# First feed-forward: a second group of seven products in place of wide forms, with PSUM seeded by ScalarE

## What is computed

```python
D_MODEL, SEQ, D_FF = 2048, 256, 5632
h = rmsnorm(x, norm_ffn[l])
x = x + (jax.nn.silu(h @ w_gate[l]) * (h @ w_up[l])) @ w_down[l]
```

## Time and profile before

| | |
|---|---|
| three runs | 2476.24, 2477.52, 2479.26 us |
| profiled execution, first to last instruction (span) | 2474.5 us |
| TensorE busy in the span | 2463.8 us, 11266 matmuls |
| VectorE / ScalarE busy | 2105.3 / 1519.2 us |
| first feed-forward, iterations | ten of 62.17 us, from about 446 to 1068 us |

### The profile page before, as it was taken

The page is one execution under the profiler, slowest core; times in us unless marked ns, Lnnn a source line. Parts: engine busy times, 40 slices in busy tenths (PEclk is TensorE's granted clock), DMA queues, the critical chain, the costliest instruction groups (busy, mean ns, idle before and its releaser), DMA issues.

```text
span 2474.5 us, 28461 instructions
## 1 busy us (share of the span) xinstructions
PE 2463.8 (100%) x11266; PEld 2040.7 (82%) x11266; DVE 2105.3 (85%) x1724; ACT 1519.2 (61%) x1448; POOL 102.3 (4%) x96
## 2 busy tenths in 40 slices
PE   9999999999999999999999999999999999999998
PEld 7888888888888888888888888888888888888887
DVE  6977667988888888978788777777799999999997
ACT  7655556566666666665565565444566667766666
POOL 0000000000000000000000000000000000000000
PEclk9999999999999999999999999999999999999999
DMA  9536446677777777775455556557557777777775
GB/s 324 186 136 235 139 153 207 216 237 235 236 236 237 235 238 238 213 251 192 151 187 172 185 204 221 176 168 247 173 194 230 232 233 232 230 230 231 229 247 161
DMA packets 262756, 524.57 MB, mean 212 GB/s; under 512 B 9248, under 2 KB 9248, under 8 KB 262368
## 3 DMA queue, kind: packets, MB, share of 16 engines
q1 hardware_dynamic: 238976, 474.56, 55.8%
q0 software_dynamic: 22784, 46.62, 10.3%
q10 hardware_dynamic: 864, 1.57, 0.2%
HBM read 478.67 MB, written 2.10 MB: 194 GB/s over the span
## 4 chain that ended last, share of the span: by engine, by line
PE 99%; DVE 1%; DMA 0%; ACT 0%; issue 0%; SPq 0%; ACTq 0%; DVEq 0%
PE acc L862 23%; PE acc L866 23%; PE acc L864 23%; PE misc L862 6%; PE misc L866 6%; PE misc L864 6%; PE acc L879 1%; PE acc L875 1%; PE acc L877 1%; PE misc L907 1%; PE misc L915 1%; PE misc L875 1%; PE misc L879 1%; PE misc L877 1%; PE misc L998 0%; PE misc L978 0%
## 5 line engine op out<-in xcount | busy, mean ns | idle before, releaser
L1917 DVE TENSOR_TENSOR w_lo<-w_raw,w_hi 128x2048 fp32r<-128x2048 f32 (+1 forms) x473 | 1059.9, 2251 | 152.4 <-ACT w_hi L1384 151.0
L1384 ACT ACTIVATE w_hi<-w_raw 128x2048 fp32r<-128x2048 f32 (+1 forms) x473 | 892.0, 1890 | 345.5 <-PE acc L866 227.6
L862 PE MATMUL acc<-w_hi,xt_hi 128*128 128x512 f32 x1132 | 447.1, 395 | 0.2
L866 PE MATMUL acc<-w_hi,xt_lo 128*128 128x512 f32 x1132 | 441.3, 390 | 0.0
L864 PE MATMUL acc<-w_lo,xt_hi 128*128 128x512 f32 x1132 | 440.6, 389 | 0.0
L862 PEld LDWEIGHTS acc<-w_hi,xt_hi 128*128 128x128 f32 x1132 | 212.6, 188 | 44.7 <-issue 1.8
L866 PEld LDWEIGHTS acc<-w_hi,xt_lo 128*128 128x128 f32 x1132 | 212.4, 188 | 44.8
L864 PEld LDWEIGHTS acc<-w_lo,xt_hi 128*128 128x128 f32 x1132 | 212.7, 188 | 42.9
L1917 DVE TENSOR_TENSOR w_lo<-w_raw_more,w_hi 128x2048 fp32r<-128x2048 f32 (+1 forms) x99 | 221.8, 2240 | 30.1 <-ACT w_hi L1384 30.1
L1384 ACT ACTIVATE w_hi<-w_raw_more 128x2048 fp32r<-128x2048 f32 (+1 forms) x99 | 186.3, 1884 | 57.5 <-DVE w_raw_more L1887 15.8
L1891 DVE TENSOR_TENSOR w_raw<-w_raw 128x2048 f32<-128x2048 f32 x80 | 182.7, 2283 | 0.0
(11 more groups left out here) (388 smaller groups left out, 4189.8 us busy)
## 6 DMA issues: line engine op xcount, KB each, us to landing
w_raw<-in_w_in SPq DMA_DIRECT2D x132, 1024.0 KB, 5.1
w_raw<-in_w_ffn_up SPq DMA_DIRECT2D x61, 1024.0 KB, 6.6
w_raw<-in_w_ffn_down SPq DMA_DIRECT2D x42, 1024.0 KB, 5.7
x<-staged POOLq DMA_DIRECT2D x80, 512.0 KB, 6.2
w_raw<-in_w_out SPq DMA_DIRECT2D x32, 1024.0 KB, 5.1
w_raw<-in_w_gate SPq DMA_DIRECT2D x32, 1024.0 KB, 6.2
w_raw<-in_w_down SPq DMA_DIRECT2D x32, 1024.0 KB, 7.3
w_raw<-in_w_up SPq DMA_DIRECT2D x27, 1024.0 KB, 5.2
```

The costliest lines, as they stand in the source:

```text
L862: nc.tensor.matmul(bank, hi[:, j, :], w_hi[:, t % RING, j, :], start=first and j == 0, stop=False, skip_group_check=shared)
L866: end = nc.tensor.matmul(bank, lo[:, j, :], w_hi[:, t % RING, j, :], start=False, stop=last and j == C - 1, skip_group_check=shared)
L1384: nc.scalar.activation(w_hi[:, t % RING, rows], raw_tile(steps[t].slot)[:, rows], ACT.Copy).then_inc(hi_ready, 1)
L1917: nc.vector.tensor_tensor(w_lo[:, t % RING, rows], raw_tile(steps[t].slot)[:, rows], w_hi[:, t % RING, rows].bitcast(F32), ALU.subtract).t ...
```

## The change

- In iterations 1 to 10 of the first feed-forward, K blocks 2 and 3 become a second full group of seven products, Q1 to Q7, on the same banks as P1 to P7. An iteration has 18 steps, 14 x 12 + 4 x 24 = 264 matmuls. VectorE makes eight weight sums, all of full size.
- `beta`, `zeta` and `gamma` no longer start from nothing: ScalarE copies `alpha` into them when P1 and Q1, then P6 and Q6, then P7 and Q7 are done (`seeds`), and the matmuls add on to that. Three matmuls before the loop (`set_bits`) mark those banks as written. VectorE's five additions become two (`second_up`, `first_up`). Silu is applied in the copy out of `beta` and `gamma`.
- x is no longer added to by DMA: ScalarE copies a quarter of x into the `acc` pair (`seed_x`), D adds on to it, and ScalarE copies the pair back to x (`x_back`), at once followed by the seed for the next quarter. `staged` and GpSimd have no part in it.
- Raw slots: seven. The sums of tokens for the second group (`q1_hi`, `q1_lo`) are made in block 0, in place of the wide ones.

```diff
-ORDER_WIDE = "P1 G3 P3 E1 D0 P5 E5 D1 E46 P6 U3 P7 P2 E73 D2 P4 D3".split()
-ORDER_WIDE_LAST = "P1 G3 E1 D0 P5 E5 U3 E46 P6 D1 E73 P2 P7 P4 P3 D2 D3".split()
+ORDER_TWO = "P1 Q1 P5 Q5 D0 P6 Q6 D1 P7 P3 Q7 Q3 D2 P2 P4 Q2 Q4 D3".split()
+ORDER_TWO_LAST = "P1 Q1 P5 Q5 D0 P6 Q6 D1 P7 Q7 P3 Q3 P2 Q2 P4 Q4 D2 D3".split()
...
-RAW_SLOTS = 6
+RAW_SLOTS = 7
+FFN_SLOTS = {1: 7, 2: 6}
...
+    def with_two_groups(order, a_weight, a_col, b_weight, b_col, down_weight, down_row):
...
+            release.update({g + "11": at[g + "4"], g + "12": at[g + "7"],
+                            g + "22": max(at[g + "3"], at[g + "6"] - 1, at[g + "7"] - 1),
+                            g + "21": max(at[g + "2"], at[g + "4"] - 1)})
...
+                sums[at[name]] = Sum(0, mine.slot, other.slot, other.count, at[name] - 1, "N" + name[1], None)
...
@@ GpSimd
-        for i in range(1, NF):
-            for n in range(Q):
-                group_read(pool, ("ffn1_down", i - 1, n))
-                k = n % 2
-                pool.dma_start(x[:, :, n * N:(n + 1) * N], staged[k][:], accum_op=ALU.add).then_inc(staged_added[k], 16)
@@ TensorE
+        def set_bits():
+            for b in range(3):
+                bank_free(b, before["sums1", 1][b])
+                nc.tensor.matmul(misc[:, b, :], xt_hi[:, 0, 0:P], xt_hi[:, 0:2, :], start=True, stop=True)
+        def seeded_iteration(i, after, within=None):
...
+                    pe.wait_ge(x_seeded, Q * (i - 1) + n + 1)
...
+                if name == "P6":
+                    pe.wait_ge(beta_seeded, i)
+                if name == "P7":
+                    pe.wait_ge(zeta_seeded, i)
+                if name == "P4":
+                    pe.wait_ge(gamma_seeded, i)
@@ ScalarE
+        def seed_x(m):
...
+            act.wait_ge(pair_read[pair], count)
+            group_read(act, ("ffn1_down", i - 2, n) if i > 1 else ("down", 3, n))
+            copy(acc[:, pair], x[:, :, n * N:(n + 1) * N]).then_inc(x_seeded, 1)
+        def x_back(i, t, n):
+            pair = pair_of(("ffn1_down", i - 1, n))
+            act.wait_ge(tile_used, t + 1)
+            copy(x[:, :, n * N:(n + 1) * N], acc[:, pair]).then_inc(pair_read[pair], 1)
+            if i < NF - 1 or n == 0:
+                seed_x(Q * (i - 1) + n + 1)
...
                 split(t + LEAD)
-                products_read(1, i, t, name, gate, hid)
+                seeds(i, t, name)
                 if k in TURNS:
                     hid_hi_half(i - 1, TURNS.index(k))
...
                 if name[0] == "D":
-                    stage_quarter(1, i, t, int(name[1]))
+                    x_back(i, t, int(name[1]))
@@ VectorE
                 split(t + LEAD)
-                results_read(1, i, t, name, gate, hid)
+                if k > 0 and order[k - 1] == "Q7":
+                    second_up(i)
+                if k > 0 and order[k - 1] == "Q3":
+                    first_up(i, t)
+                if i < NF - 1 and name == "D3":
+                    gated_sums(i)
                 if k in TURNS:
                     hid_lo_half(i - 1, TURNS.index(k))
```

More of the change, by code:

```diff
@@ L92, in two_ahead @@
         return "P7", "E5", "E73"
-    return ("P7",) if order is ORDER_WIDE_LAST else ()
+    return ()
 def last_of(order, *names):
@@ L1124, in pair_step @@
             products(t, [(banks[letter], hi, lo)], first=new, shared=True)
+        def set_bits():
[3 more added lines that the diff above has]
+        def seeded_iteration(i, after, within=None):
+            stage, order = ("ffn1", i), order_of(1, i)
+            sums_key = (*stage, "sums")
+            alpha, epsilon = pair_banks(pair_of(sums_key))
+            banks = {"1": alpha, "6": alpha, "7": alpha, "5": epsilon, "2": misc[:, 0, :], "4": misc[:, 1, :],
+                     "3": misc[:, 2, :]}
+            for k, name in enumerate(order):
+                t = STEP[stage, name]
+                if name[0] == "D":
+                    n = int(name[1])
+                    key = ("ffn1_down", i - 1, n)
+                    if n == 0:
+                        ht_ready(i - 1)
+                    pe.wait_ge(x_seeded, Q * (i - 1) + n + 1)
+                    products(t, both(pair_banks(pair_of(key)), ht_hi, ht_lo), first=False, shared=True,
+                             between=within and within.get(name))
+                    after(k, name)
+                    continue
+                form = name[1]
+                if name == "P1":
+                    pair_free(sums_key)
+                if name == "P6":
[4 more added lines that the diff above has]
+                    pe.wait_ge(gamma_seeded, i)
+                if form in "5673":
+                    pe.wait_ge(s_lo_done, S_PHASES.index("ffn1" if name[0] == "P" else "ffn1q") + 1)
+                    s_hi, s_lo = (s1_hi, s1_lo) if name[0] == "P" else (q1_hi, q1_lo)
+                    hi, lo = s_hi[:, S_FORMS["P" + form]], s_lo[:, S_FORMS["P" + form]]
+                else:
+                    b = (0 if form == "1" else 1) + (0 if name[0] == "P" else 2)
+                    cs, rows = slice(C * b, C * b + C), second if form == "4" else first
+                    hi, lo = xt_hi[:, cs, rows], xt_lo[:, cs, rows]
+                products(t, [(banks[form], hi, lo)], first=name in ("P1", "P5"), shared=True)
+                after(k, name)
         def ffn_iteration(ffn, i, s_hi, s_lo, ready, after, within=None):
@@ L1143, in ffn_iteration @@
                         ready(i - 1)
-                    products(t, both(pair_banks(pair_of(key)), *((ht_hi, ht_lo) if ffn == 1 else (h2_hi, h2_lo))),
-                             between=within and within.get(name))
+                    products(t, both(pair_banks(pair_of(key)), h2_hi, h2_lo), between=within and within.get(name))
                 else:
@@ L2513, in _ @@
             if k == 5:
-                wide_lo_piece(2)
+                wide_lo_piece(1)
                 taps_on(0, "a", 0)
```

170 lines of the change are left out of this document (123 added, 47 removed).

## The result

The changed kernel takes 2502.53 us (median of four runs, 2502.37 to 2503.73) against 2477.46 before: a ratio of 1.0102, 95% interval 1.0088 to 1.0117. It is slower, as forecast, but by 25 us and not by 7. The span of the profiled execution is 2501.8 us, 27.3 more than before; that is more than the 25 of the medians, because the profiled execution was here the slowest of the four (2503.73 us) and, by its span, the fastest (2476.24 us) of the kernel before.

The account below looks back on a forecast made before the run. The prediction took TensorE to bound the kernel, with VectorE having about 10% left. Its terms, -13.6 + 0.7 + 19.5 + 0.6 = +7.2 us, moved the median from 2477.5 to 2484.7, range 2472 to 2498.

Parts of the forecast that it names:

- TensorE's saving: Six matmuls fewer in each of ten iterations, 60 at 0.2267 us: -13.6 us.
- VectorE's sum: VectorE's own work in one iteration of the changed kernel: 60.9 us, against TensorE's 60.8.
- The loop through D1: Gate product, half turn, D1, copy to x, seed, Q3's rounding, VectorE's work to the next gate product: 62.98 us per iteration.
- the second rival: The seed is cheap or partly overlaps: iteration near 62.2, result 2474 to 2482, no change that can be told; chance 0.18.
- The failed step: TensorE's wait of 2.17 us at the first half turn, in nine iterations: +19.5 us.
- The fourth rival: TensorE's clock falls at its 2.2 us stands: up to 2.7 us more each, 2509; chance 0.05 together with the fifth rival.
- Iteration 1: Gate product ends at 447.6, the turn comes at 448.6, so the first iteration was to have no wait.
- The last iteration: In its own order P4's remainder comes at 42.4, TensorE reaches it at 41.8: one more delay, +0.6 us.
- The other loops: Paths through D0, D2, D3 and the seeds of `beta`, `zeta`, `gamma`, taken as shorter than the one through D1.
- D1's load: D1's weight tile takes D0's slot at 7.2 and is wanted at 12.6; landing at 12.8 was to cost nothing.
- the third rival: D1's load lands late in some or all iterations: up to 9 x 2.3 us more, 2490 to 2506; chance 0.12.
- the fifth rival: The saving of TensorE's matmuls isn't there: +13.6 us, 2498; chance 0.05 together with the fourth rival.

Follow-up runs that it names:

- e4: The kernel before, with five of the six matmuls of step E5 left out in each of ten iterations: 2465.03 us against 2477.03.
- e2: The changed kernel with nine idle matmuls ahead of TensorE's wait at the first half turn, iterations 2 to 10: 2489.55 us, ratio 1.0051.
- e8: The changed kernel with two idle matmuls ahead of TensorE's wait at the first half turn: 2489.78 us, ratio 1.0049.
- e10: The changed kernel, with ScalarE's copy to x and seed after D1, D2 and D3 moved behind the next rounding: 2507.35 us, ratio 1.0120.
- e7: The changed kernel, with VectorE's weight sums for P4 and Q4 cut to 64 columns: 2484.13 us, ratio 1.0028.
- e3: The changed kernel, with VectorE making the gate product before the sum for Q5 and the remainder of P5: 2488.98 us, ratio 1.0046.
- e5: The changed kernel, with VectorE's gate product and the first half of `ht_lo` both made earlier: 2487.51 us, ratio 1.0042.
- e13: The changed kernel, with copies to x, seeds and VectorE's sums for P4 and Q4 all cut to 64 columns: 2476.35 us, ratio 0.9997.
- e6: The changed kernel, with gate product and first half of `ht_lo` earlier, and D2's seed behind Q3's rounding: 2482.97 us, ratio 1.0023.
- e1: The changed kernel, with D2's seed of x moved behind the rounding of Q3 on ScalarE: 2485.33 us, ratio 1.0032.

## Why the prediction was wrong in size and right in direction

- *TensorE's saving*, -13.6: right (e4: 0.23 per matmul by the iteration, 0.24 by the medians, where 0.2267 was taken).
- *VectorE's sum*, 60.9: right (61.08 in the windows).
- *The loop through D1*, 62.98: right but for 0.18 (63.16 in e2 and e8, where the clock stays up). The copies of 1.03, the idle time of 2.0 at Q3, the wait of 2.17 (measured 2.13) are all there. The seed, which the trace of before did not have, measured 0.97 from start to start, near the 0.92 taken and far from both of its bounds; the second rival's cheap seed is out. (In the walk, 25.71 and a copy of 1.03 make 26.74 and not 26.76, which changes nothing.)
- *The failed step* is the price of that wait. "TensorE waits 62.98 - 60.81 = 2.17 at the turn" was put into the sum as 2.17 and no more. The matmuls behind it were costed at 0.2267 each, a spacing measured where TensorE never stands. The runs show 0.43 for over 3 us behind each of the nine stands: 1.57 us more each, 14 us in all. The fourth rival said so and priced it well, up to 2.7 an iteration and 2509 in all; it was given a share of 0.05 with another, and the range ended at 2498. The rows of before had no wait of this length, so they bore on it in neither direction, and a chance so small had nothing behind it. With the 14 us the forecast would have been 2499; the wait of iteration 1 (2.1) and the loop's 0.18 nine times (1.6) bring it to the measured 2502.5. That the direction came out right owes nothing to the clock: the loop of 63.16 alone gives the 2489.6 of e2, 0.5% over before. The Trainium skill (TensorE: Matmul & The Clock Gate, Part 1) has the clock fall to half after an idle stretch and come back after sustained work; the windows at 839 to 845 agree, with 0.50 and then 1.00, though not every stand had such a fall behind it (e10).
- *Iteration 1*, "so it does not wait": wrong by 2.1. The time 447.6 was taken from the trace of before, where VectorE makes this product directly behind TensorE's last result; in the changed kernel two weight sums and two remainders stand ahead of it, as the prediction itself says for the other iterations. The hedge in the text ("if they are done before P5") was also a right question. VectorE finishes block 0's token sums at 442.2, makes those four without a gap until 451.0, and ends the product at 452.4. No run tells the share of the token sums from that of the order.
- *The last iteration*, +0.6: measured 0.8.
- *The other loops are "shorter"*: right, but by 0.4 to 0.5 only (D2 alone 62.64 in e7; 62.80 in e3, where TensorE waits for bank 3, and in e5, where it waits at D0). That fits with no single edit that computes everything bringing more than this once the clock was up.
- *D1's load*: ScalarE rounds D1 (851.67) directly behind its copy to `hid` and does not wait for the load; the third rival is out:

```profile
851.10 0.67 ACT L1467 ACTIVATE hid<-acc,rstd 128x512 f32<-128x512 f32 x1
851.67 1.91 ACT L1464 ACTIVATE w_hi<-w_raw_more 128x2048 fp32r<-128x2048 f32 x1
```

- *The saving isn't there*: e4 gained 12.0 us, so the fifth rival is out. The Trainium skill (Perfetto Trace Analysis, Identifying the Most-Contended Engine) would have given e4 no gain as the prediction read it, by weight loads alone; the section names a second measure beside them, the share of the peak FLOPs (MFU), which the prediction left out.

So the large change moves the time the wrong way for reasons of different weight. The copies to x and the seeds stand in ScalarE's queue ahead of roundings (63.16 to 61.84 without their length); the seed is new there, while a copy of the same size, to `staged`, stood there before. VectorE has little slack left to take that up (61.08 of work against TensorE's 60.8), but this weighs less by itself: 4 us less of its work brought 0.52 with the copies in place (e7) and nothing with short ones (e13). And behind the stand that follows, TensorE's clock fell nine times of nine (64.72 against 63.16). The best version that computes everything, e6, is still 0.23% slower than the kernel before.

## What to carry to other kernels

When a change takes work from the bounding engine and puts it on engines with "slack", walk the loop through all of their queues: a signal that goes once around three in-order engines sets the iteration though none of them is full, and next to it lie other loops, nearly as long. Price a new stand of TensorE twice, once for its length and once for the matmuls behind it at half clock, with a chance that is not small. Where such a stand can't be avoided, two idle matmuls in it gave back 13 us here.

## What was not expected of the hardware

- Stands of TensorE of 2.13 us (nine of nine in the kernel after) and 2.23 (one in e3) were followed by matmuls at 1.2 GHz; those of 1.65 to 1.7 (e1, e7, e8) and 1.82 to 2.04 (e3) were not. Among the longer ones it was not the length that decided: of those of 2.08 to 2.19 in iteration 1 three of thirteen were followed by the low clock, of those of 2.69 in e10 seven of nine. The time at half clock, 840 to 843.5 in the windows above, cost 1.57.
- ScalarE writes 128x1024 from SBUF to PSUM in 1.03 us, the same as the other way (1.03 at 866.55 and at 867.61).
